# Cross attention's queries as two units of two heads, with the first heads' steps beside the second unit

## What is computed

```python
hx = rms_norm(x, g_cross); hm = rms_norm(mem, g_mem)
cq = rms_norm((hx @ w_cq).reshape(B, T, 4, 128), g_cq)   # 2048 -> 512
ck = rms_norm((hm @ w_ck).reshape(B, M, 4, 128), g_ck)
cv = (hm @ w_cv).reshape(B, M, 4, 128)
s = einsum('bthd,bmhd->bhtm', cq, ck)
x = x + einsum('bhtm,bmhd->bthd', softmax(s), cv).reshape(B, T, -1) @ w_co
```

## Time and profile before

| | us |
|---|---|
| median of three runs | 2412.4 |
| the profiled execution | 2409.67 |
| its span, first to last instruction | 2408.4 |
| TensorE busy | 2395.4 |
| VectorE busy | 1491.3 |
| ScalarE busy | 1122.1 |
| HBM read | 449 MB, 187 GB/s |

### The profile page before, as it was taken

One profiled execution on the slowest core, in us unless ns is written; L12 is line 12 of the kernel. 1 busy time (PEld: TensorE's weight loads), 2 busy tenths in 40 slices (PEclk: granted clock), 3 DMA queues, 4 the chain that ended last, 5 costly groups with the idle time before them and its releaser, 6 DMA issues.

```text
span 2408.4 us, 28130 instructions
## 1 busy us (share of the span) xinstructions
PE 2395.4 (99%) x11328; PEld 1986.7 (82%) x11328; DVE 1491.3 (62%) x2119; ACT 1122.1 (47%) x1410; POOL 0.2 (0%) x4
## 2 busy tenths in 40 slices
PE   9999999999999999999999999999999999999999
PEld 8888888888888888888888887887888888888887
DVE  5565999865544545576667866876555555554443
ACT  5454444544443444454555555546444444444333
POOL 0000000000000000000000000000000000000000
PEclk9999999999999999999999999999999999999999
DMA  7645666656665765666544445554565665566664
GB/s 265 205 143 184 192 192 193 212 192 210 195 193 160 251 228 192 195 215 191 177 149 156 168 139 180 179 181 137 186 192 186 190 192 186 190 192 188 202 203 141
DMA packets 124942, 452.96 MB, mean 188 GB/s; under 512 B 13771, under 2 KB 15996, under 8 KB 123788
## 3 DMA queue, kind: packets, MB, share of 16 engines
q1 hardware_dynamic: 124812, 451.17, 58.1%
HBM read 448.99 MB, written 2.12 MB: 187 GB/s over the span
## 4 chain that ended last, share of the span: by engine, by line
PE 97%; DVE 1%; DMA 1%; ACT 1%; issue 0%; SPq 0%; ACTq 0%
PE ps L1256 30%; PE ps L1258 30%; PE ps L1257 30%; PE ps L773 2%; PE ps L806 1%; PE ps L1118 1%; PE ps L787 1%; DMA t_raw<-w_in 1%; PE ps L797 0%; DVE t_wlo L2490 0%; PE ps L917 0%; PE ps L1288 0%; ACT t_whi L1743 0%; PE ps L1101 0%; PE ps L1022 0%; PE ps L885 0%
## 5 line engine op out<-in xcount | busy, mean ns | idle before, releaser
L2490 DVE TENSOR_TENSOR t_wlo<-t_raw,t_whi 128x1024 fp32r<-128x1024 f32 (+1 forms) x806 | 983.0, 1223 | 802.5 <-ACT t_whi L1743 799.3
L1743 ACT ACTIVATE t_whi<-t_raw 128x1024 fp32r<-128x1024 f32 x804 | 850.0, 1059 | 1016.4 <-PE ps L1258 997.1
L1256 PE MATMUL ps<-t_whi,t_A 128*128 128x512 f32 (+1 forms) x2496 | 986.2, 395 | 2.2 <-DVE t_wlo L2490 2.2
L1258 PE MATMUL ps<-t_wlo,t_A 128*128 128x512 f32 (+1 forms) x2496 | 969.8, 389 | 0.0
L1257 PE MATMUL ps<-t_whi,t_A 128*128 128x512 f32 (+1 forms) x2496 | 968.4, 388 | 0.0
L1256 PEld LDWEIGHTS ps<-t_whi,t_A 128*128 128x128 f32 x2496 | 469.2, 188 | 99.9 <-issue 5.7
L1258 PEld LDWEIGHTS ps<-t_wlo,t_A 128*128 128x128 f32 x2496 | 468.8, 188 | 97.8
L1257 PEld LDWEIGHTS ps<-t_whi,t_A 128*128 128x128 f32 x2496 | 469.5, 188 | 90.9
L1256 PE MATMUL ps<-t_whi,t_Y0a 128*128 128x512 f32 x576 | 225.2, 391 | 0.0
L1258 PE MATMUL ps<-t_wlo,t_Y0a 128*128 128x512 f32 x576 | 224.2, 389 | 0.0
L1257 PE MATMUL ps<-t_whi,t_Y0a 128*128 128x512 f32 x576 | 224.1, 389 | 0.0
(11 more groups left out here) (317 smaller groups left out, 1229.7 us busy)
## 6 DMA issues: line engine op xcount, KB each, us to landing
t_raw<-w_in SPq DMA_DIRECT2D x375, 512.0 KB, 3.9
t_raw<-w_gu SPq DMA_DIRECT2D x176, 512.0 KB, 3.6
t_raw<-w_down SPq DMA_DIRECT2D x88, 512.0 KB, 4.1
t_raw<-w_branch SPq DMA_DIRECT2D x64, 512.0 KB, 4.0
t_raw<-w_out SPq DMA_DIRECT2D x64, 512.0 KB, 3.7
t_raw<-w_ck SPq DMA_DIRECT2D x16, 512.0 KB, 4.1
t_raw<-w_cv SPq DMA_DIRECT2D x16, 512.0 KB, 4.3
t_raw<-w_cq SPq DMA_DIRECT2D x8, 512.0 KB, 3.5
```

What stands on the lines that cost most here:

```text
L1256: te.matmul(ps[:, 0:n], u.op.hi[:, x, tok], h[:, k, :], start=(kt == 0), stop=False)
L1258: made = te.matmul(ps[:, 0:n], u.op.hi[:, x, tok], l[:, k, :], start=False, stop=(kt == u.kts - 1))
L1743: se.activation(whi[:, k % NH, 0:n], raw[:, d % NR, 0:n], ACT.Copy).then_inc(*hi.up((d, 1)))
L2490: ve.tensor_tensor(wlo[:, k % NH, p], raw[:, d % NR, p], whi[:, k % NH, p].bitcast(F32), ALU.subtract).then_inc(*lo.up(name))
```

## The change

- `cq` becomes `cq0` (chunks 541 to 544) and `cq1` (545 to 548), 256 columns, that is two heads, each; the weights `w_cq` are packed accordingly, four key tiles to a chunk.
- `cross_q`, `cross_rms` and `cross_out` take an index. The steps of the first two heads (`cross_q0`, `cross_rms0`, `cross0`, `cross1`) are placed in the chunks 544 to 548, beside `cq1`. `cross_out0`, `cross_q1`, `cross_rms1` and the scores of `cross2` and `cross3` come at the end of chunk 548 and ahead of chunk 549.
- The chunks of `wc0` and `wc1` are interleaved: 549 is the first half of `wc0`'s keys (the first two heads), 550 the first half of `wc1`'s, 551 and 552 the second halves. The rest of `cross2` and `cross3` stands in 549 and 550, `cross_out1` ahead of 551.
- The last steps of `cross_in` move ahead within chunk 542, those of `ffn_in` and `ffn_norm` go with the chunks in which `wc0` and `wc1` now end.
- The tile for exponentials and transposed tiles (`LX`) moves from region Y0a to region A, since the operand of `cq1` still lies in Y0a. `ffn_norm` gets a wait of ScalarE on its own earlier square.

The rest of the diff passes the index on, on each engine.

```diff
+        54214],
     cross_norm=[52814, 53214, 53614, 54014, 54014],
-    cross_q=[54814, 54814, 54820, 54820],
-    cross_rms=[54814, 54820],
-    cross0=[54826, 54827, 54830, 54831, 54834, 54835],
-    cross1=[54826, 54827, 54831, 54832, 54834, 54835],
-    cross2=[54823, 54824, 54828, 54829, 54833, 54834],
-    cross3=[54826, 54827, 54833, 54834, 54835, 54836],
-    cross_out=[54836, 54837, 54900, 54901],
-    ffn_in=[55102, 55114, 55202, 55214, 55314, 55400, 55501, 55502, 55614, 55700, 55802, 55814, 55914, 56000, 56101,
+    cross_q0=[54414, 54500, 54502, 54504],
+    cross_rms0=[54414, 54500, 54504, 54506],
+    cross0=[54506, 54601, 54704, 54706, 54801, 54803],
+    cross1=[54600, 54603, 54714, 54802, 54804, 54806],
+    cross_out0=[54814, 54820],
+    cross_q1=[54814, 54820, 54821, 54822],
+    cross_rms1=[54814, 54820, 54821, 54822],
+    cross2=[54821, 54823, 54914, 55000, 55002, 55014],
+    cross3=[54823, 54824, 55001, 55002, 55014, 55020],
+    cross_out1=[55021, 55022],
+    ffn_in=[55202, 55214, 55302, 55314, 55400, 55402, 55501, 55502, 55614, 55700, 55802, 55814, 55914, 56000, 56101,
         56102, 57302, 57314, 57402, 57414, 58902, 58914, 59002, 59014, 60502, 60514, 60602, 60614, 62102, 62114,
         62202, 62214, 63702, 63714, 63802, 63814, 65302, 65314, 65402, 65414, 66902, 66914, 67002, 67014, 68502,
...
-    LX = at("Y0a", [8, 512])
+    LX = at("A", [8, 512])
...
-    unit("cq", dr["w_cq"], 512, 16, cop, "cq", lambda t: cqs[:, t, :])
+    for i in range(2):
+        unit(f"cq{i}", dr["w_cq"][i], 256, 16, cop, "cq", lambda t, i=i: cqs[:, t, 256 * i:256 * i + 256])
...
+    def crossed(one, other):
+
+        a = next(i for i, x in enumerate(chunks) if x[0].name == one)
+        assert chunks[a + 3][0].name == other and chunks[a + 1][0].name == one
+        chunks[a + 1], chunks[a + 2] = chunks[a + 2], chunks[a + 1]
+
+    crossed("wc0", "wc1")
...
-        def cross_q():
+        def cross_q(i):
             for t in range(NT):
-                ps = take(4 + t)
-                pe.wait_ge(*kept.at(("cq", t)))
-                for h in range(4):
-                    made = te.transpose(ps[:, h * P:(h + 1) * P], cqs[:, t, h * P:(h + 1) * P], ident)
-                made.then_inc(*cq_s["pe"].up(f"t{t}"))
-                free[4 + t] = cq_s["act"].at(f"t{t}")
-                yield
-                yield
-
-        def cross_rms():
-            yield
-            yield
...
+        def cross_rms(i):
+            for j in range(4):
+                yield
...
-        def cross_q():
-            to = cqT[:].rearrange("p a (b n) -> p b a n", b=2)
+        def cross_q(i):
             for t in range(NT):
                 yield
-                act.wait_ge(*cq_s["pe"].at(f"t{t}"))
+                act.wait_ge(*cq_s[i]["pe"].at(f"t{t}"))
                 act.wait_ge(*gla_s["dve"].at("ck"))
-                se.activation(to[:, :, :, t * P:(t + 1) * P], banks[4 + t][:].rearrange("p (b a n) -> p b a n", b=2, a=2),
-                              ACT.Copy, scale=par("g_cq")).then_inc(*cq_s["act"].up(f"t{t}"))
-                yield
-
-        def cross_rms():
-            yield
-            root(cr_s, "var", "root", cqr[:])
+                o = i * 256 + t * P
+                se.activation(cqT[:, :, o:o + P], banks[4 + 2 * i + t][:, 0:256].rearrange("p (b n) -> p b n", b=2),
+                              ACT.Copy, scale=par("g_cq")).then_inc(*cq_s[i]["act"].up(f"t{t}"))
+                yield
+
+        def cross_rms(i):
+            yield
+            yield
+            root(cr_s[i], "var", "root", cqr[:, 4 * i:4 * i + 4])
+            yield
             yield
...
-            rows = cqr[:, 4 * t + g0:4 * t + g0 + 2]
+            rows = cqr[:, 2 * i:2 * i + 2]
...
-        def cross_out():
-            for i in range(2):
-                yield from rounded(coop_s, (2 * i,), coop, lambda j: 4 + 2 * i)
+        def cross_out(i):
+            yield from rounded(coop_s, (2 * i,), coop, lambda j: 4 + 2 * i)
...
                 act.wait_ge(*joined.at((f"wc{n}", 1)))
+                if n:
+                    act.wait_ge(*fn_s["act"].at(f"sq{n - 1}"))
...
-        def cross_rms():
-            r = cqr[:]
+        def cross_rms(i):
+            r = cqr[:, 4 * i:4 * i + 4]
             for t in range(NT):
-                x3 = cqs[:, t, :].rearrange("p (h d) -> p h d", d=P)
-                dve.wait_ge(*kept.at(("cq", t)))
-                ve.tensor_tensor(csq[:, 4 * t:4 * t + 4, :], x3, x3, ALU.mult).then_inc(*dve_step.up())
+                x3 = cqs[:, t, 256 * i:256 * i + 256].rearrange("p (h d) -> p h d", d=P)
+                dve.wait_ge(*kept.at((f"cq{i}", t)))
+                q = csq[:, 4 * t + 2 * i:4 * t + 2 * i + 2, :]
+                ve.tensor_tensor(q, x3, x3, ALU.mult).then_inc(*dve_step.up())
                 dve.wait_ge(*dve_step.last())
-                ve.tensor_reduce(r[:, 4 * t:4 * t + 4], csq[:, 4 * t:4 * t + 4, :], AX, ALU.add).then_inc(*dve_step.up())
+                ve.tensor_reduce(r[:, 2 * t:2 * t + 2], q, AX, ALU.add).then_inc(*dve_step.up())
+                if t == 0:
+                    yield
             dve.wait_ge(*dve_step.last())
-            ve.tensor_scalar(r, r, 1.0 / P, RMS_EPS, ALU.mult, ALU.add).then_inc(*cr_s["dve"].up("var"))
-            yield
-            dve.wait_ge(*cr_s["act"].at("root"))
-            ve.reciprocal(r, r).then_inc(*cr_s["dve"].up("r"))
+            ve.tensor_scalar(r, r, 1.0 / P, RMS_EPS, ALU.mult, ALU.add).then_inc(*cr_s[i]["dve"].up("var"))
+            yield
+            yield
+            dve.wait_ge(*cr_s[i]["act"].at("root"))
+            ve.reciprocal(r, r).then_inc(*cr_s[i]["dve"].up("r"))
             yield
```

More of the change, by code:

```diff
@@ L438, in body @@
     cn_s = signals("cn", "", "root", "var r")
-    cq_s = signals("cq", "t0 t1", "t0 t1")
-    cr_s = signals("cr", "", "root", "var r")
+    cq_s = [signals(f"cq{i}", "t0 t1", "t0 t1") for i in range(2)]
+    cr_s = [signals(f"cr{i}", "", "root", "var r") for i in range(2)]
     cross_s = [signals(f"cross{i}", "scores turned product", "exp out", "max sum copy") for i in range(4)]
@@ L1182, in cross_norm @@
                 yield
-        def cross_q():
+        def cross_q(i):
             for t in range(NT):
-                ps = take(4 + t)
-                pe.wait_ge(*kept.at(("cq", t)))
-                for h in range(4):
-                    made = te.transpose(ps[:, h * P:(h + 1) * P], cqs[:, t, h * P:(h + 1) * P], ident)
-                made.then_inc(*cq_s["pe"].up(f"t{t}"))
-                free[4 + t] = cq_s["act"].at(f"t{t}")
+                b = 4 + 2 * i + t
+                ps = take(b)
+                pe.wait_ge(*kept.at((f"cq{i}", t)))
+                for k in range(2):
+                    h = 2 * i + k
+                    made = te.transpose(ps[:, k * P:(k + 1) * P], cqs[:, t, h * P:(h + 1) * P], ident)
+                made.then_inc(*cq_s[i]["pe"].up(f"t{t}"))
+                free[b] = cq_s[i]["act"].at(f"t{t}")
                 yield
                 yield
-        def cross_rms():
-            yield
-            yield
+        def cross_rms(i):
+            for j in range(4):
+                yield
         def cross(i):
@@ L1203, in cross @@
                 LX[:, 2 * i, :], LX[:, 2 * i + 1, :], lambda h, k: ckv[1][:, k, (g0 + h) * P:(g0 + h + 1) * P],
-                [cq_s["act"].at(f"t{t}")], reader="act", copier="dve")
-        def cross_out():
-            for i in range(2):
-                yield from turns(coop_s, (2 * i,), (4 + 2 * i,), tiles_of(co),
-                                 [cross_s[2 * i]["act"].at("out"), cross_s[2 * i + 1]["act"].at("out")])
+                [cq_s[i // 2]["act"].at(f"t{t}")], reader="act", copier="dve")
+        def cross_out(i):
+            yield from turns(coop_s, (2 * i,), (4 + 2 * i,), tiles_of(co),
+                             [cross_s[2 * i]["act"].at("out"), cross_s[2 * i + 1]["act"].at("out")])
         def ffn_in():
@@ L1225, in tensor_program @@
             gla=gla(), gla_ahead=gla_ahead(), gla_norms=gla_norms(), nsa_part0=nsa_part(0), nsa_part1=nsa_part(1),
-            cross_in=cross_in(), cross_norm=cross_norm(), cross_q=cross_q(), cross_rms=cross_rms(), cross0=cross(0),
-            cross1=cross(1), cross2=cross(2), cross3=cross(3), cross_out=cross_out(), ffn_in=ffn_in(),
-            ffn_norm=ffn_norm()))
+            cross_in=cross_in(), cross_norm=cross_norm(), cross_q0=cross_q(0), cross_rms0=cross_rms(0), cross0=cross(0),
+            cross1=cross(1), cross_out0=cross_out(0), cross_q1=cross_q(1), cross_rms1=cross_rms(1), cross2=cross(2),
+            cross3=cross(3), cross_out1=cross_out(1), ffn_in=ffn_in(), ffn_norm=ffn_norm()))
         filled = {}
@@ L1781, in evacuate @@
                 act.wait_ge(*cn_s["dve"].at("r"))
-                made = se.activation(u.dst(t), ps[:], ACT.Copy, scale=keepers[:, 4 + t:5 + t])
+                made = se.activation(u.dst(t), ps[:, 0:u.n], ACT.Copy, scale=keepers[:, 4 + t:5 + t])
```

(5 more changed lines are left out.)

28 lines of the change are left out of this document (13 added, 15 removed).

## The result

The changed kernel takes 2418.49 us (median of 11 runs, 2413.47 to 2420.11) against 2411.97 us of the kernel before in the same session (11 runs, 2406.01 to 2414.59). The ratio is 1.0026, with a 95% interval of 1.0018 to 1.0033: 4.3 to 8.0 us slower, in any case within 0.5%. The profiled execution took 2413.47 us for a span of 2412.2 us.

The account below looks back on a forecast made before the run. TensorE bounds the kernel, busy 2395.4 of 2408.4 us. Cross attention 5.5 + 0.4 + 11.95 = 17.85 us against 15.26 gives +2.6, the pitch +1.2: 2412.4 + 3.8 = 2416.2 us, range 2407 to 2422.6.

Parts of the forecast that it names:

- all four cases: Whole kernel: forecast 2416.2 us (chance 0.55), waits covered 2409.6 (0.25), first heads stalled 2418.3 (0.12), clock loss 2419.6 (0.08).
- the second rival: Beside cq1: first heads' steps stall its products, each waiting behind a weight split; +5.9 us, 2418.3 us, chance 0.12.
- my three signs of being wrong: Stretch's idle time below 3 us; ScalarE's second-tile copy not waiting behind the root; another stretch of the kernel moving.
- M: Time at which the last product of cq1 is issued, read in the traces as the end of its pitch.
- The pitch: Query products: 192 matmuls 0.12 us apart instead of 96 at 0.227, +1.2 us, called certain.
- First heads: Beside cq1: 5.5 us of small matmuls and switches plus 0.4 us of wait, bounds 0 and 2.5 us.
- Last heads, front: After cq1: TensorE waits 1.6 and 1.75 us for ScalarE's query copies, the second queued behind the root.
- Last heads, tail: Before chunk 551: 0.9 us wait for output scaling behind the split of 554, then 1.7 us of waiting, unchanged.
- Chunks 551 to 557: After cross attention: chunks keep their cover, ffn_in steps move with their chunks; cost nothing.
- The clock: Waits between M+0.9 and M+5.1: rival that the granted clock falls, 3.4 us lost, 2419.6 us, chance 0.08.

Follow-up runs that it names:

- the units alone: Kernel before with only the queries split into two units of 256 columns, all cross attention steps behind both; 2410.52 us against 2411.64, ratio 1.0000.
- the filler kernel: Changed kernel plus 12 and 13 unread identity transposes ahead of the scores of the third and fourth step; 2416.41 us against 2411.64, ratio 1.0021.
- the second trace: The changed kernel run once more with nothing altered; 2419.79 us against 2412.97 of the kernel before, ratio 1.0026.

## Why the prediction was right, and where not

The forecast was 2416.2 us, 3.8 more than before; measured are 2418.49 and 6.5 more by the medians, 5.5 by the distances. The range held it, and the sign and the mechanism were right: what the change hides is less than what it adds. The range by itself confirms little, since it is wide enough for all four cases, and that 2418.49 lies beside the 2418.3 of the second rival is chance: its mechanism didn't occur. One of my three signs of being wrong came true: another stretch of the kernel moved, 551 to `fg0`, by 0.74 us. The other two did not: TensorE was idle 5.2 us between M and chunk 551, and the copy of the second tile did wait behind the root. The granted clock, forecast at 1.00, fell.

- **The pitch.** 192 matmuls at 0.12 us against 96 at 0.227: forecast +1.2, measured +1.21, of which 0.16 come back behind the last product.
- **First heads.** Forecast 5.5 us of small work and a wait of 0.4 us; measured 5.23 us in sum (29.13 from the first query product to M, less the 23.90 of the units alone), with a wait of 0.21. The small work was priced some 0.5 us too high: a group of scores costs 0.86 us and not 1.0 (1626.26 to the second product behind it at 1627.24, less a pitch). The second rival (stalled products in `cq1`) didn't happen.
- **Last heads, front.** Forecast starts of the scores at M+2.5 and M+5.1, measured the same. The profile's idle time is 1.36 and 1.47 us for the forecast 1.6 and 1.75, which I counted from the issue of the work ahead and not from its end. The reason stated for the second wait, a root placed ahead of the copy, was tested: the wait left with the order. But the gain didn't stay whole; 0.73 us came back at the next step.
- **Last heads, tail.** Forecast 0.9 us and 1.7 us of wait, measured 0.86 and 1.51 (1.50 in the kernel before). The size was right and my reason for the first was wrong: the split of chunk 554 delays the scaling by 0.05 us at most, the rest is the scaling's own time. With the clock full chunk 551 starts at M+17.74 (the filler kernel), 0.3 us later than forecast.
- **Chunks 551 to 557.** The step that failed: "TensorE has no wait there now, and the steps of `ffn_in` move with their chunks; nothing". They didn't move evenly. With the ends of `wc0` and `wc1` in neighbouring chunks three groups of transposes that share one bank start within 5.6 us (1664.07, 1667.26, 1669.70) instead of 7.1 us before, and TensorE loses 0.62 of the 0.74 us to it.
- **The clock.** I priced a fall at 3.4 us, gave it 8 in 100 and tied it to a wait near 3.11 us. It fell behind two waits of 1.36 and 1.47 us with four score records between them, for 3.4 us, which cost 1.42 us by the filler kernel (801.25 - 799.83), 1.64 in the second trace. My 3.4 us of loss were worked out from an episode twice as long. The place was right; that it takes a wait near 3.11 us was not.

The sum of the measured terms: 1.21 for the pitch, 0.62 for the bank, 1.42 for the clock, and 2.27 that are left for waits and switches in cross attention, where I had forecast 2.6. The last is a remainder, but the traces give it once more: 5.23 us for the first heads, and 17.74 - 5.44 = 12.30 for the last two with the clock full (forecast 5.9 and 11.95), make 17.53 against 15.26. The waits alone grew by 5.4 - 3.4 = 2.0 us. So the terms that I had in the sum came to 3.5 instead of 3.8, and the two that I had at nothing, or as a rival, made 2.0.

The Trainium skill ("ScalarE: Activation LUTs", section "What ACT_TABLE_LOAD costs") counts a drain of 1.38 us with each load and doesn't say on which side of it; by my estimate from that figure the sum would have been 0.6 us larger. ScalarE's rows after show both switches: the load for the root starts 0.02 us after the copy ends, the next one 0.01 us after the copy, and the exponential 0.02 us after its end, each load 1.28 us. The trace doesn't agree with the drain here.

## What to carry to other kernels

Look for what stands beside each step. Beside the products of `cq1` the steps of the first heads cost 0.21 us of wait. At the front of the second chain, with no product beside it, TensorE waited 1.36 us for a step queued behind a weight split and 1.47 us for one queued behind a root; with the steps ahead of both 2.34 us of that went and 1.34 came back at the next steps, and at the tail the place of the split was worth 0.05 us. So a wait taken away in front is no gain before the next one is looked at. Before cutting a wide unit in two to gain cover, price the cut itself (here 1.2 us of at most 4.2) and the switches, and look whether a new order of the same steps gives the cover without it: the wide unit with interleaved chunks, another order and two banks was 1.2 us better than before and 6.7 us better than the change. After a move, look behind it as well: steps that come closer together share a bank that had been enough. All this is one kernel; that it carries over is not shown.

## What was not expected of the hardware

Two waits of TensorE of 1.36 and 1.47 us, with four score records between them, were followed by 3.4 us at 1.2 GHz in both traces of the changed kernel, while the kernel before, with waits of 0.34, 0.68, 0.44, 0.44 and 1.50 us and more small matmuls between them, kept 2.4 GHz in both of its traces. 25 transposes that compute nothing, put into the waits, gave back 1.4 us, in one trace.
